# Moving the last pair's gates behind the down products of pair 14, and building the first pair's tokens by a one-hot product

## The chip, the cores and the metric

The kernel runs on one core of a Trainium2 chip. The metric is the device time of one launch in microseconds (us); the median of several runs is used. The core's engines are TensorE (PE; its weight loads are shown as PEld), VectorE (DVE), ScalarE (ACT), GpSimd (POOL) and SyncE (SP), and 16 DMA engines move data between HBM, SBUF and back. Each engine works through its own program in order; a wait on a semaphore holds up all that stands behind it on that engine.

## What is computed

One layer of a hybrid decoder on 320 tokens (256 of a prompt, 64 of eight short samples): a norm, a mixer (convolution group and state-space group), a residual, then a norm and a two-level mixture of experts, a residual and a final norm. The part that this change touches is the mixture of experts. Cut to that, in float32 throughout:

```python
def hier_moe(h, rg_w, rg_b, re_w, re_b, w_gate, w_up, w_down):
    lg = tf @ rg_w + rg_b                                # 4 groups
    grp = argmax(lg); g1 = softmax(lg)[grp]
    le = (tf @ re_w + re_b)[grp]                         # 8 experts of that group
    top_v, top_i = top_k(le, 2); g2 = softmax(top_v)
    eid = grp * 8 + top_i
    combine = sum(one_hot(eid, 32) * (g1 * g2))
    for e in range(32):
        hid = silu(t @ w_gate[e]) * (t @ w_up[e])        # 1024 -> 512
        acc = acc + combine[:, e:e + 1] * (hid @ w_down[e])   # 512 -> 1024
```

## The kernel before

**Tiling.** The tokens are three tiles of 128, 128 and 64 rows (TILES). Experts are worked in 16 pairs (pair i holds experts 2i and 2i + 1). Each expert takes up to 64 of its tokens, so a pair fills 128 rows. For one pair: POOL gathers the normed rows of its 128 slots from HBM (hn_scratch) by an index column; PE transposes them (tokens_T, L1196) into two PSUM banks and DVE multiplies them by the norm's gain into xgt; PE makes the gate and up products of both experts (gate_up, L1213 and L1214, eight k each); ACT takes the silu (L1581), DVE multiplies (L1654); PE transposes the product (hidden_T, L1225), ACT copies it (L1599); PE makes the down products (L1236; the very last expert in halves, L1246), ACT copies their rows into yo (rows_back, L1587); PE adds them to the tokens' places with a one-hot matrix (to_tile, L1261; combine_most has five tiles of six, combine_rest the last).

**Order on PE.** In iteration i stand: gates 2i, combine_most(i - 2), gates 2i + 1, tokens of pair i + 1, combine_rest(i - 2), downs of pair i - 1, hidden_T(i). After the loop come combine 14, then the downs of experts 30 and 31 and the last adds. So the downs of pair 14 stand behind the gates of pair 15.

**Weights.** SP loads 96 blocks of 2 MB (gate, up or down of one expert) in the order of expert_units() into 11 places (e_slot), round and round. Block j may be loaded once block j - 11 is used (gu_done, dn_done). The first eleven lie where the mixer's data lay, so their loads wait for the end of that: block 7 for the out product of the samples (filled, outs), block 8 for the last router logits (lg2), the two halves of block 9 for the normed rows being in HBM (hn_out) and the first gather being issued (gath_begun), block 10 for kept, the last residual rows that PE reads from the same place. Blocks 11 and 12 are loaded in halves, the first halves when half of the first gate product is through (gu_half).

**Choice of experts.** DVE finds the group and the two experts by first_max (maximum, equality times a descending count, maximum, equality). Then "chosen" lets PE count the tokens of each expert (counts, L1157) into the bank "rank". From these DVE makes `first`, a one-hot matrix of tokens against the 128 slots of pair 0, PE multiplies it by the token numbers (L1172), DVE makes an index of it and POOL gathers pair 0. Meanwhile DVE computes the weights and osel, PE the indices of all other pairs (slot_values, L1180), which DVE reads into gpair and others.

**Banks.** MOE_JOBS lists the PSUM jobs of the experts in order; job n lies in bank n mod 3 and waits until job n - 3 has been read.

## Time and profile before

| | before |
|---|---|
| median of 3 runs | 792.37 us (791.98 to 793.82) |
| span of the profiled execution | 789.4 us |
| PE busy | 757.8 us (96%) |
| DVE / ACT / POOL busy | 270.5 / 154.4 / 140.3 us |
| moved by DMA | 249.58 MB, mean 316 GB/s |

The span is the time from the first to the last instruction in the profile of one execution. PE's busy share is that of pipelined matmuls with modelled ends. The clock column ("PEclk") is the clock that was granted to PE, 1.00 for 2.4 GHz and 0.50 for 1.2 GHz. Idle time of an engine is given with what ended it; "issue" stands where the profile shows no releaser.

### The profile page before, as it was taken

The numbers are of one execution on the slowest core, as the hardware profiler recorded it, in microseconds if no ns is written. First come the engines' busy times: TensorE is split into PE (matmuls) and PEld (weight loads), VectorE is DVE, ScalarE is ACT, GpSimd is POOL, SyncE is SP. The second block draws the span as 40 slices with busy tenths as digits, with TensorE's granted clock in tenths as the row PEclk, the third lists the DMA queues.
The fourth block names the chain that finished last, engine by engine and source line by source line (L and its number), as shares of the span: only waits on it lengthen the run. The fifth ranks groups of instructions, "written<-read, shape, count | busy, mean of one in ns | idle before, by whom it ended". The sixth has DMA issues, their size and how long they took to land.

```text
span 789.4 us, 8694 instructions
## 1 busy us (share of the span) xinstructions
PE 757.8 (96%) x3470; PEld 360.5 (46%) x3470; DVE 270.5 (34%) x629; ACT 154.4 (20%) x308; POOL 140.3 (18%) x168
## 2 busy tenths in 40 slices
PE   6999999999999999799999999999999999989896
PEld 4667677767843335434333333333333333333332
DVE  2399499985656423511101101110110011011003
ACT  3211121245712003202011112101111110110122
POOL 2279998612002000100000000000000000000000
PEclk9999999999999999799999999999999999999998
DMA  9990610042659786999999999999999999999982
GB/s 312 304 364 10 230 40 1 9 107 108 188 213 275 252 306 237 368 374 414 429 426 427 425 429 425 425 430 426 427 427 426 425 426 427 427 429 425 429 356 69
DMA packets 51400, 249.58 MB, mean 316 GB/s; under 512 B 6982, under 2 KB 24422, under 8 KB 38671
## 3 DMA queue, kind: packets, MB, share of 16 engines
q1 hardware_dynamic: 45460, 243.40, 77.2%
q10 hardware_dynamic: 3371, 2.81, 1.2%
q0 software_dynamic: 2528, 2.79, 1.1%
q8 instruction: 29, 0.48, 0.2%
q14 instruction: 12, 0.10, 0.0%
HBM read 246.87 MB, written 8.61 MB: 324 GB/s over the span
## 4 chain that ended last, share of the span: by engine, by line
PE 91%; DMA 3%; DVE 2%; SPq 2%; issue 2%; ACT 1%; POOLq 0%; DVEq 0%
PE bank L1213 28%; PE bank L810 18%; PE bank L1236 14%; PE bank L1076 9%; PE bank L1261 9%; DMA xcx<-in_state_conf_conv 2%; PE bank L1196 2%; SPq L491 1%; PE bank L1225 1%; PE bank L1065 1%; PE bank L1034 1%; PE bank L905 1%; PE bank L1214 1%; PE bank L1122 1%; PE bank L1047 0%
## 5 line engine op out<-in xcount | busy, mean ns | idle before, releaser
L810 PE MATMUL bank<-region_a,ring 128*128 128x320 f32 x576 | 157.2, 433 | 1.0 <-DMA ring<-in_w_in 1.0
L1654 DVE TENSOR_TENSOR region_a<-region_a,bank 64x512 f32<-64x512 f32 (+1 forms) x33 | 22.5, 680 | 377.6 <-ACT region_a L1581 377.6
L1214 PE MATMUL bank<-ring,zz 128*64 128x512 f32 x320 | 145.4, 610 | 0.0
L1213 PE MATMUL bank<-ring,zz 128*64 128x512 f32 x288 | 127.3, 595 | 2.7 <-issue 2.7
L810 PEld LDWEIGHTS bank<-region_a,ring 128*128 128x128 f32 x576 | 108.7, 190 | 46.3 <-DVE region_a L1654 1.1
L1655 DVE SCALAR_TENSOR_TENSOR bank<-region_a,par,bank 128x256 f32<-128x256 f32 x232 | 91.2, 479 | 0.0
L763 POOL DMA_INDIRECT region_a<-hn_scratch,region_a x16 | 15.9, 996 | 369.6 <-PE bank L1196 355.8
L1261 PE MATMUL bank<-zz,masks 128*128 128x512 f32 (+1 forms) x192 | 77.2, 603 | 0.7 <-ACT zz L1587 0.7
L1213 PEld LDWEIGHTS bank<-ring,zz 128*64 128x64 f32 x288 | 38.1, 137 | 82.5 <-issue 81.7
L1076 PE MATMUL bank<-ring,x_v_y 128*128 128x512 f32 (+1 forms) x192 | 74.0, 605 | 0.0
L1581 ACT ACTIVATE region_a<-bank 64x512 f32<-64x512 f32 x32 | 18.9, 590 | 271.5 <-PE bank L1214 271.5
L1587 ACT ACTIVATE zz<-bank 64x512 f32<-64x512 f32 x60 | 35.5, 591 | 106.7 <-PE bank L1236 106.3
L1236 PE MATMUL bank<-ring,xcx 128*64 128x512 f32 x240 | 53.8, 596 | 0.0
L1076 PEld LDWEIGHTS bank<-ring,x_v_y 128*128 128x128 f32 (+1 forms) x192 | 26.7, 171 | 43.3 <-issue 43.0
L1261 PEld LDWEIGHTS bank<-zz,masks 128*128 128x128 f32 (+1 forms) x192 | 26.6, 172 | 39.1 <-issue 39.1
L1214 PEld LDWEIGHTS bank<-ring,zz 128*64 128x64 f32 x320 | 43.4, 140 | 0.0
L674 POOL TENSOR_TENSOR x_v_y<-x_v_y 128x512 f32<-128x512 f32 x29 | 36.8, 1270 | 2.3
L1213 PE MATMUL bank<-x_v_y,zz 128*64 128x512 f32 x80 | 35.4, 595 | 0.5 <-issue 0.5
L1236 PEld LDWEIGHTS bank<-ring,xcx 128*64 128x64 f32 x240 | 16.5, 137 | 35.8 <-issue 35.8
L1213 PE MATMUL bank<-xcx,zz 128*64 128x512 f32 x64 | 30.8, 638 | 2.0 <-issue 2.0
L672 POOL TENSOR_TENSOR x_v_y<-region_a,par 128x512 f32<-128x512 f32 x30 | 32.2, 1074 | 2.2
L1214 PE MATMUL bank<-x_v_y,zz 128*64 128x512 f32 x64 | 28.3, 595 | 0.0
(313 smaller groups left out, 770.1 us busy)
## 6 DMA issues: line engine op xcount, KB each, us to landing
ring<-in_expert_w_up SPq DMA_DIRECT2D x20, 2048.0 KB, 24.4
ring<-in_expert_w_gate SPq DMA_DIRECT2D x17, 2048.0 KB, 30.3
ring<-in_expert_w_down SPq DMA_DIRECT2D x16, 2048.0 KB, 34.8
ring<-in_w_in SPq DMA_DIRECT2D x9, 2048.0 KB, 15.7
x_v_y<-in_expert_w_down SPq DMA_DIRECT2D x6, 2048.0 KB, 33.5
x_v_y<-in_expert_w_gate SPq DMA_DIRECT2D x5, 2048.0 KB, 34.6
ring<-in_w_out SPq DMA_DIRECT2D x4, 2048.0 KB, 10.0
xcx<-in_expert_w_gate SPq DMA_DIRECT2D x4, 2048.0 KB, 31.8
```

The costliest lines, as they stand in the source:

```text
L672: link(pool.tensor_tensor(tmp4, u_seq[:, :, :, k:k + TB], w4(par, k, NC), ALU.mult))
L674: return link(pool.tensor_tensor(acc, acc, tmp4, ALU.add))
L810: ins = pe.matmul(pt[0:m, 0:T], w[:, k, :], ht[:, k, :], start=k == 0, stop=k == KD - 1)
L1076: return pe.matmul(dst, mix, w, start=c == 0, stop=c == 2 * NC - 1)
L1213: pe.matmul(to[0:CAP, :], x[:, k, :], wg[:, FE * k:FE * k + FE], **st)
L1214: ins = pe.matmul(to[CAP:P, :], x[:, k, :], wu[:, FE * k:FE * k + FE], **st)
L1236: ins = pe.matmul(to[CAP * q:CAP * q + CAP, :], x[:, k, :], wd[:, D * k + 512 * q:D * k + 512 * q + 512], start=k == 0, stop=k == 3)
L1261: return pe.matmul(dst, rows[:, t0:t0 + n], of[q][0:rows.shape[0], :], start=False, stop=end)
L1581: act.activation(sil[b], job_bank("gate", e)[0:CAP, :], ACT.Silu).then_inc(S("sil"), 1)
L1587: ins = act.activation(yo[own_half[e % 2], 512 * q:512 * q + 512], pt[CAP * q:CAP * q + CAP, :], ACT.Copy)
L1654: tt_ = lambda out, a, b, op: dve.tensor_tensor(out, a, b, op)
L1655: stt = lambda out, a, s_, b, op0, op1: dve.scalar_tensor_tensor(out=out, in0=a, scalar=s_, in1=b, op0=op0, op1=op1)
```

## The change

There are two groups of edits. In the tail, iteration 15 is taken out of PE's loop: after hidden_T(14) come combine 13, the downs of pair 14, combine 14, then the gates of pair 15, hidden_T(15) and the last downs. ACT's order, the order of the weight blocks and the list of bank jobs follow. The four gate and up blocks of pair 15 are loaded in halves, and a gate product waits for the second halves at k = 4 only.

In front, pair 0 is no longer gathered. PE multiplies the normed rows hn (in SBUF) by the one-hot `first`: for each of eight k and three token tiles one product of 128x128. The job "first" goes, and "slots" gets bank 1; all expert jobs lie two banks further. SP loads the second half of block 9 before it waits for lg2, and the first half behind hn_out and xg_T 2. residual(1, [1]) moves ahead of the product. On DVE, three small operations in first_max become two, the subtractions for the two exponentials come after "chosen", osel is made before the weights, and the tokens of pair 0 are scaled before the indices are read. tee and osel move to another place in SBUF.

```diff
@@ expert_units
-        units += [(m, 2 * i + j) for j in range(2) for m in range(2)]
-        if i:
-            units += [(2, 2 * i - 2), (2, 2 * i - 1)]
+        downs = [(2, 2 * i - 2), (2, 2 * i - 1)] if i else []
+        gates = [(m, 2 * i + j) for j in range(2) for m in range(2)]
+        units += downs + gates if i == LAST else gates + downs
@@ SP
-            sp_.wait_ge(filled, J[("lg2",)] + 1)
-            load_expert(n_slot - 3)
...
+            load_half(n_slot - 2, 1, S("tenth_half"))
+            sp_.wait_ge(filled, J[("lg2",)] + 1)
+            load_expert(n_slot - 3)
             sp_.wait_ge(S("hn_out"), 48)
-            load_half(n_slot - 2, 0, S("tenth_half"))
-            sp_.wait_ge(S("gath_begun"), 1)
-            load_half(n_slot - 2, 1, expert_in[n_slot - 2])
+            sp_.wait_ge(S("xg_T"), 2)
+            load_half(n_slot - 2, 0, expert_in[n_slot - 2])
             sp_.wait_ge(S("kept"), 1)
             load_expert(n_slot - 1)
...
+            for e in (NE - 2, NE - 1):
+                pair_of = (E_AT[0, e], E_AT[1, e])
+                for j in pair_of:
+                    place_free(j)
+                    load_half(j, 0, S(f"late_half{e % 2}"))
+                for j in pair_of:
+                    load_half(j, 1, expert_in[j % n_slot])
@@ POOL
-            for i in range(NE // 2):
-                wait(pool, S("xg_T"), 2 * i)
+            for i in range(1, NE // 2):
+                if i > 1:
+                    pool.wait_ge(S("xg_T"), 2 * i)
@@ PE, front
-            pe.wait_ge(S("first"), 1)
-            pt = take(pe, "first")
-            for r in range(3):
-                n = TILES[r][1]
-                ins = pe.matmul(pt[:, 0:1], first[0:n, r, :], tokid[0:n, r:r + 1], start=r == 0, stop=r == 2)
-            ins.then_inc(filled, 1)
             residual(1, [1]).then_inc(S("kept"), 1)
+            pe.wait_ge(S("hn"), 3)
+            pe.wait_ge(S("first"), 1)
+            after_read(pe, "h2", 2, 1)
+            after_read(pe, "lg2")
+            for h in range(2):
+                to = job_bank("tokens", (0, h))
+                for k in range(4):
+                    for r in range(3):
+                        n = TILES[r][1]
+                        ins = pe.matmul(to[:, P * k:P * k + P], hn[0:n, r, 4 * h + k:D:KD], first[0:n, r, :],
+                                        start=r == 0, stop=r == 2)
+                ins.then_inc(S("xg_T"), 1)
@@ PE, tail
+            combine_most(LAST - 2)
+            combine_rest(LAST - 2)
+            expert_down(NE - 4)
+            expert_down(NE - 3)
+            combine_most(LAST - 1)
+            combine_rest(LAST - 1)
+            for e in (NE - 2, NE - 1):
+                pe.wait_ge(S(f"late_half{e % 2}"), 32)
+                gate, up = (e_slot[E_AT[m, e] % n_slot] for m in range(2))
+                to = job_free(pe, "gate", e)
+                pe.wait_ge(S("xgt"), 2 * LAST + 2)
+                gate_up(to, xgt[:, :, own_half[e % 2]], gate, up, late=e).then_inc(S("gu_done"), 1)
+            hidden_T(LAST)
             over = pe.value_load(mcount[0:1, 0:1], min_val=0, max_val=T)
@@ ACT
             for i in range(NE // 2):
+                if i == LAST:
+                    rows_back(2 * i - 2)
+                    rows_back(2 * i - 1)
                 silu(2 * i)
                 silu(2 * i + 1)
-                if i:
+                if 0 < i < LAST:
@@ DVE, first_max
-                for r in range(3):
-                    ins = stt(tmp_[:, r, :], vals[:, r, :], col(mx)[:, r:r + 1], desc, ALU.is_equal, ALU.mult)
-                link(ins)
+                link(tt_(tmp_, vals, wide(mx, w), ALU.is_equal))
+                link(tt_(tmp_, tmp_, bc(desc.unsqueeze(1), [P, 3, w]), ALU.mult))
```

The program order on PE in front, from the counts (s_chosen) to the first gate product. Before:

```order
L1157 MATMUL bank<-region_a,masks 128x96 [waits s_dve_read,s_chosen]
...
L1147 MATMUL bank<-x_v_y,ident 64x512 [waits s_x2]
...
L1172 MATMUL bank<-region_a,zz 128x1 [waits s_dve_read,s_first]
L1172 MATMUL bank<-region_a,zz 128x1 x2
L1147 MATMUL bank<-x_v_y,ident 128x512 [waits s_x2]
L1180 MATMUL bank<-region_a,zz 64x64 [waits s_dve_read,s_osel]
L1180 MATMUL bank<-region_a,zz 64x64 x11
L1196 MATMUL bank<-ident,region_a 128x128 [waits s_gath,s_act_read,s_dve_read]
L1196 MATMUL bank<-ident,region_a 128x128 x7
L1213 MATMUL bank<-xcx,zz 64x512 [waits s_expert_in1,s_xgt,s_expert_in0,s_dve_read]
```

And in the changed kernel (all lines are some 10 to 20 further down):

```order
L1167 MATMUL bank<-region_a,masks 128x96 [waits s_dve_read,s_chosen]
...
L1190 MATMUL bank<-zz,x_v_y 128x128 [waits s_dve_read,s_first,s_hn]
L1190 MATMUL bank<-zz,x_v_y 128x128 x23
L1198 MATMUL bank<-region_a,zz 64x64 [waits s_dve_read,s_osel]
L1198 MATMUL bank<-region_a,zz 64x64 x11
L1233 MATMUL bank<-xcx,zz 64x512 [waits s_expert_in1,s_expert_in0,s_xgt,s_dve_read,s_act_read]
```

The one-column product and the 8 transposes are gone; 24 products of 128x128 stand ahead of the slots product, and both residual products ahead of these.

On SP at the same place, blocks 7 to 10 and the first of block 11. Before:

```order
L503 DMA ring<-in_expert_w_up 128x4096 [waits s_filled]
L503 DMA region_a<-in_expert_w_down 128x4096 [waits s_filled]
L561 DMA x_v_y<-in_expert_w_down 128x2048 [waits s_hn_out]
L561 DMA x_v_y<-in_expert_w_down 128x2048 [waits s_gath_begun]
L503 DMA x_v_y<-in_expert_w_gate 128x4096 [waits s_kept]
L561 DMA xcx<-in_expert_w_up 128x2048 [waits s_gu_half]
```

In the changed kernel:

```order
L506 DMA ring<-in_expert_w_up 128x4096 [waits s_filled]
L562 DMA x_v_y<-in_expert_w_down 128x2048
L506 DMA region_a<-in_expert_w_down 128x4096 [waits s_filled]
L562 DMA x_v_y<-in_expert_w_down 128x2048 [waits s_xg_T,s_hn_out]
L506 DMA x_v_y<-in_expert_w_gate 128x4096 [waits s_kept]
L562 DMA xcx<-in_expert_w_up 128x2048 [waits s_gu_half]
```

One half of block 9 moved ahead of block 8, the other waits for the token product, and block 10 stands behind it.

On PE in the tail, from hidden_T(14) on; L1225 is hidden_T, L1213 a gate product, L1261 a combine, L1236 and L1246 downs. Before:

```order
L1225 MATMUL bank<-ident,region_a 128x128 x3
L1213 MATMUL bank<-xcx,zz 64x512 [waits s_yo,s_xgt,s_expert_in1,s_expert_in0]
...
L1213 MATMUL bank<-ring,zz 64x512 [waits s_yo,s_xgt,s_expert_in3,s_expert_in2]
...
L1236 MATMUL bank<-region_b,xcx 64x512 [waits s_hidt,s_expert_in4]
...
L1236 MATMUL bank<-ring,xcx 64x512 [waits s_hid,s_hidt,s_expert_in5]
...
L1225 MATMUL bank<-ident,region_a 128x128 [waits s_hid]
...
L1261 MATMUL bank<-zz,masks 64x512 [waits s_yo,s_places]
...
L1308 TENSOR_LOAD region_a
...
L1236 MATMUL bank<-ring,xcx 64x512 [waits s_yo,s_hidt,s_expert_in6]
```

In the changed kernel, with L1245 for hidden_T, L1233 for a gate product, L1281 for a combine, L1256 for downs:

```order
L1245 MATMUL bank<-ident,region_a 128x128 x3
L1281 MATMUL bank<-zz,masks 64x512 [waits s_yo,s_places]
...
L1256 MATMUL bank<-xcx 64x512 [waits s_yo,s_hidt,s_expert_in0]
...
L1256 MATMUL bank<-ring,xcx 64x512 [waits s_yo,s_hidt,s_expert_in1]
...
L1281 MATMUL bank<-zz,masks 64x512 [waits s_yo,s_places]
...
L1233 MATMUL bank<-ring,zz 64x512 [waits s_xgt,s_hidt,s_late_half0]
...
L1233 MATMUL bank<-region_b,zz 64x512 [waits s_xgt,s_yo,s_late_half1]
...
L1245 MATMUL bank<-ident,region_a 128x128 [waits s_hid,s_yo]
...
L1336 TENSOR_LOAD region_a
...
L1256 MATMUL bank<-ring,xcx 64x512 [waits s_hid,s_hidt,s_expert_in6]
```

The gates of pair 15 moved behind the downs of pair 14 and combine 14, and nothing but hidden_T and a register load stands between them and the last downs.

## Rows read from the trace of the kernel before

**Rows 1.** The page: DMA busy tenths in 40 slices; the software queue (gathers).

```profile
DMA  9990610042659786999999999999999999999982
...
q0 software_dynamic: 2528, 2.79, 1.1%
```

**Rows 2.** Stretches: us, PE, PEld, DVE, ACT, POOL busy; PEclk, DMA share, GB/s.

```profile
313.00:325.50 12.50, 9.68 (x62) 6.76 (x61) 8.58 (x41) 5.58 (x8) 0.22 (x1) 0.96 0.94 357
...
326.00:328.00 2.00, 1.83 (x2) 0.25 (x2) 1.80 (x9) 0.00 (x0) 0.98 (x1) 0.50 0.83 233
328.00:337.00 9.00, 7.73 (x48) 4.53 (x50) 3.05 (x14) 0.00 (x0) 1.24 (x3) 0.62 1.03 421
337.00:340.50 3.50, 3.50 (x20) 1.29 (x18) 0.00 (x0) 0.00 (x0) 0.00 (x0) 1.00 0.67 186
340.50:360.00 19.50, 18.50 (x91) 7.69 (x88) 3.71 (x6) 2.37 (x4) 0.99 (x1) 1.00 1.01 413
360.00:640.00 280.00, 279.59 (x1235) 100.40 (x1232) 32.32 (x54) 41.99 (x71) 10.82 (x11) 1.00 1.01 426
640.00:762.00 122.00, 114.96 (x490) 41.65 (x488) 11.15 (x19) 16.80 (x29) 2.04 (x3) 0.97 1.01 427
```

**Rows 3.** Timeline: start, us, engine, line; first gate records behind waits.

```profile
648.75 1.00 PE L1213 MATMUL bank<-region_b,zz 128*64 128x512 f32 x1 [1.90 <-issue]
...
708.37 0.61 PE L1213 MATMUL bank<-ring,zz 128*64 128x512 f32 x1 [2.69 <-issue]
...
737.73 1.09 PE L1213 MATMUL bank<-xcx,zz 128*64 128x512 f32 x1 [1.99 <-issue]
```

**Rows 4.** DMA issues at 696.07: the up block of expert 30, us to landing.

```profile
ring<-in_expert_w_up SPq DMA_DIRECT2D x1, 2048.0 KB, 41.6
```

**Rows 5.** Timeline and one line's view: hand-overs and register load in the tail.

```profile
735.11 1.19 ACT L1587 ACTIVATE zz<-bank 64x512 f32<-64x512 f32 x2 [2.24 <-PE bank L1236]
...
757.12 0.59 ACT L1581 ACTIVATE region_a<-bank 64x512 f32<-64x512 f32 x1 [10.07 <-PE bank L1214]
757.74 0.69 DVE L1654 TENSOR_TENSOR region_a<-region_a,bank 64x512 f32<-64x512 f32 x1 [9.90 <-ACT region_a L1581]
...
765.19 1.19 ACT L1587 ACTIVATE zz<-bank 64x512 f32<-64x512 f32 x2 [2.24 <-PE bank L1236]
766.41 0.60 ACT L1599 ACTIVATE xcx<-bank 128x512 f32<-128x512 f32 x1
766.53 4.71 PE L1261 MATMUL bank<-zz,masks 128*64 128x512 f32 x12 [0.70 <-ACT zz L1587]
...
L1308 PEldq TENSOR_LOAD <-region_a x1: 481/481/481, 766.6 to 766.6; - x1
```

**Rows 6.** Timeline in front: choice, counts, residual, SP's loads, first gate.

```profile
318.85 0.50 DVE L1655 SCALAR_TENSOR_TENSOR region_a<-region_a 128x8 f32<-128x8 f32 x3
...
321.00 1.10 DVE L1654 TENSOR_TENSOR region_a<-region_a 128x24 f32<-128x24 f32 x6
...
321.82 1.66 PE L1157 MATMUL bank<-region_a,masks 128*128 128x96 f32 x12 [2.59 <-DVE region_a L1654]
323.41 1.08 PE L1147 MATMUL bank<-x_v_y,ident 64*64 64x512 f32 x4
...
325.21 3.38 SPq L561 DMA_DIRECT2D x_v_y<-in_expert_w_down  x2
...
332.95 1.09 PE L1213 MATMUL bank<-xcx,zz 128*64 128x512 f32 x1
...
337.54 0.33 SPq L561 DMA_DIRECT2D xcx<-in_expert_w_up  x1
```

**Rows 7.** Groups by line and shape, PE, 195 to 240 us: busy us, mean ns.

```profile
L1034 PE MATMUL bank<-ident,ring 128*128 128x128 f32 x64 | 7.6, 275 | 0.8 <-DVE x_v_y L1813 0.8
...
L1013 PE MATMUL bank<-xcx,ring 128*128 128x128 f32 x16 | 1.9, 275 | 0.0
```

**Rows 8.** One stretch, columns as in Rows 2.

```profile
738.00:740.50 2.50, 2.50 (x8) 0.73 (x7) 0.00 (x0) 0.00 (x0) 0.00 (x0) 0.50 1.00 426
```

More of the change, by code:

```diff
@@ L147, in bank_table @@
     fixed = {("yos",): 2, ("mean",): 3, ("h2", 2, 0): 1, ("h2", 2, 1): 2, ("lg2",): 0, ("rank",): 1,
-             ("first",): 0, ("slots",): 2}
+             ("slots",): 1}
     aside = {J[("mean",)]: [("mean",)], J[("h0T", 0, 0)]: [("yos",)], J[("yoT",)]: OUT_JOBS, J[("h2", 0, 0)]: [("lg",)]}
-    for name in (("h2", 2, 0), ("h2", 2, 1), ("lg2",), ("rank",), ("first",), ("slots",)):
+    for name in (("h2", 2, 0), ("h2", 2, 1), ("lg2",), ("rank",), ("slots",)):
         aside[J[name]] = [name]
@@ L188, in moe_jobs @@
     for i in range(NE // 2):
+        jobs += down(i - 1) if i == LAST else []
         jobs += [("gate", 2 * i + j, "hid", 2 * i + j + 1) for j in range(2)]
-        jobs += tokens(i + 1) if i + 1 < NE // 2 else []
-        jobs += down(i - 1) if i else []
+        jobs += tokens(i + 1) if i < LAST else []
+        jobs += down(i - 1) if 0 < i < LAST else []
         jobs += [("hidden", i, "hidt", i + 1)]
@@ L1185, in _ @@
             pe.wait_ge(S("osel"), 1)
-            slot_values(take(pe, "slots")).then_inc(filled, 1)
-            after_read(pe, "first")
+            slot_values(take(pe, "slots"), osel).then_inc(filled, 1)
             pe.wait_ge(free["act"], len([1 for _, who in JOBS if who == "act"]))
@@ L1212, in gate_up @@
                         pe.wait_ge(S("xgt"), 2)
+                    if late is not None and k == 4:
+                        expert_landed(pe, 0, late)
+                        expert_landed(pe, 1, late)
                     pe.matmul(to[0:CAP, :], x[:, k, :], wg[:, FE * k:FE * k + FE], **st)
@@ L1294, in _ @@
                     gate_up(to, xgt[:, :, own_half[e % 2]], gate, up, first=e == 0).then_inc(S("gu_done"), 1)
-                more = i + 1 < NE // 2
-                if more:
-                    pe.wait_ge(S("gath"), 16 * (i + 2))
-                    for h in range(2):
-                        tokens_T(i + 1, h)
+                pe.wait_ge(S("gath"), 16 * (i + 1))
+                for h in range(2):
+                    tokens_T(i + 1, h)
                 if i >= 2:
@@ L1967, in _, with tokens @@
             link(tt_(col(M_W2), col(M_W1), col(M_E), ALU.mult))
[L1968 to L1979 removed]
+            tt_(val[:, :, :, 1, :], ee, bc(cols[:, M_W1:M_W2 + 1, :].unsqueeze(3), [P, 2, 3, NE]), ALU.mult)\
+                .then_inc(S("osel"), 1)
+            def tokens(i, h):
+                dve.wait_ge(S("xg_T"), 2 * i + h + 1)
+                src = job_bank("tokens", (i, h))
+                tt_(xgt[:, 4 * h:4 * h + 4, :], src[:, :].rearrange("p (k s) -> p k s", k=4),
+                    bc(lnffn[:, 4 * h:4 * h + 4].unsqueeze(2), [P, 4, P]), ALU.mult).then_inc(S("xgt"), 1)
+            for h in range(2):
+                tokens(0, h)
             link(dve.tensor_reduce(cols[:, M_T, 0:1], cnt, AX.X, ALU.max))
@@ L2017, in tokens_more @@
                            bc(lnffn[:, :].unsqueeze(2), [P, KD, CAP]), ALU.mult)
-            for h in range(2):
-                tokens(0, h)
             def places(b, tok, w):
```

76 lines of the change are left out of this document (31 added, 45 removed).

## The prediction

> **What bounds the kernel now.** I read the slices of the page first. From the 18th slice on the DMA engines stand at 9 of 10 and never leave it until the last weights are in [rows 1]. The table of stretches gives the rate: 426 and 427 GB/s from 360 to 762 us [rows 2]. One pair of experts needs six weight blocks of 2.10 MB, 12.6 MB, so 29.5 us. TensorE (PE) is busy nearly all the time too, so the second question is which of the two waits. Until 640 us it is not PE: 279.59 of 280 us busy [rows 2]. Behind that its idle times come before the first gate product of a pair, 1.90 us at 648.75, 2.69 at 708.37 and 1.99 at 737.73, with "issue" as releaser, which is how a wait for a landed weight block looks here [rows 3]. The starts at 708.37 and 737.73 lie 29.36 us apart, the time of one pair on the DMA engines. So from 646 us on the weight stream sets the pace, and whatever delays the stream in the first 340 us delays 708.37 by as much, since there is no gap in it afterwards to make it up. After 737.73 nothing waits for a weight again, and PE's own work and its hand-overs with ACT and DVE set the end. Check of the reading: the up block of expert 30 is issued at 696.07 and lands 41.6 us later, at 737.7 [rows 4].
>
> Two places therefore count: how early the stream is without holes (312 to 340 us), and PE's chain from 735.7 us on. The edits are costed as what they do to these two.
>
> **Front: the choice.** Each of the three first_max calls swaps three small operations in one group (0.50 us) for two that wait for each other, about 0.18 + 0.04 us each [rows 6]: 0.44 instead of 0.53 with its gap, 0.27 us over three. Two subtractions of 3 or 12 columns leave the path to "chosen", about 0.1 us each, as they ran back to back with their neighbours. For the six in a row at 321.00 that is 1.10/6 = 0.18 as an upper bound [rows 6]. PE's counts, at 321.82 before [rows 6], start near 321.35.
>
> **Front: the tokens of pair 0.** The gather, 3.8 us from issue, the 8 transposes and the one-column product go. In their place stand 24 products of 128x128 in float32, three token tiles for each of eight k. Nearest row: L1013, non-transposed float32 128x128, two records to a matmul, 16 records in 1.9 us, so 0.119 a record [rows 7]. 48 records are 5.7 us at full clock. Ahead of them PE does the counts (1.6 us from 321.82 to 323.41 [rows 6]), residual(2) (1.08 with its tail, about 1.0 to the next [rows 6]) and now also residual(1, [1]), which is two more steps of 512 columns like those two, 0.9 us. The one-hot is two DVE operations behind the counts, under 1 us by the gap from 323.41 to PE's next work before, so DVE is ready before PE is. Product: from 321.35 + 1.6 + 1.0 + 0.9 = 324.8 to 330.5. Slots product (24 records, 1.0 to 1.7 us), which the gates wait for, then about 1.3 us of DVE reads: gates start near 333.0, as before (332.95 [rows 6]), but without the half clock that before had from 325.5 on [rows 2]. PE has 1.9 us of slack at 648.75 anyway, so this start is covered, and pays only from 2 us of delay on.
>
> A page of the Trainium skill has a rule against this trade. TensorE: Matmul & The Clock Gate, Terms, says that transpose mode makes float32 four times as fast as a matmul. The transposes L1034 take 0.119 us each and the matmuls L1013 0.238 [rows 7], a factor of two here, so the trace does not bear the rule out.
>
> **Front: the stream.** This is the term that matters. SP now issues the second half of block 9 right behind block 7 (312.2), no longer behind hn_out and the gather's start. But the first half now waits for xg_T 2, the end of the product, because it lands on the normed rows that the product reads. Block 10 stands behind it in SP's queue though its own condition is met earlier. Their issue was at 325.21 and right after 328.1; it becomes 330.6 for both. Bytes moved by 340.5 us, before: 12.5 us x 357 + 2 x 233 + 9 x 421 + 3.5 x 186 GB/s = 4.46 + 0.47 + 3.79 + 0.65 = 9.37 MB [rows 2], less one gather of 2.79/16 = 0.17 MB [rows 1], 9.2 MB. After: blocks 7, 8, half of 9 and the last hn rows, 5.5 MB, done near 327; then nothing until the restart. What a restart costs I take from 325.21: no packet before 326.0, then 233 GB/s for 2 us, a lag of 0.8 + 0.9 = 1.7 us. So as if at full rate from 332.3; (340.5 - 332.3) x 0.427 = 3.5 MB, sum 9.0 MB. The second restart of before (337.54 [rows 6], 186 GB/s) is gone: half a block and block 10 last until 339.8, and the next halves, bound to half of the first gate product, are issued near 336.6. The lack of 0.2 to 0.3 MB at 427 GB/s is **+0.6 us**. Bounds: a ramp half as long, DVE a little faster and a gather hidden give -0.4; a chain later by 0.5 us and restarts as before give +1.5.
>
> **Tail: what goes.** Order before from 735.74: wait 1.99 for the blocks of expert 30, gates 30 (low clock at first), combine 13 and gates 31, downs 28 and 29, hand-over 0.70, combine 14 and downs 30 and 31. The same products stand in the new order, so they cancel. Removed: the wait 1.99 [rows 3]; the low clock, 737.7 to 741.0 at 0.50 [rows 8], where 3.3 us give 1.65 us of work, so 1.65; the wait 0.70 before combine 14 with 0.07 beside it [rows 5]. Sum 4.4 us.
>
> **Tail: what comes.** (a) combine 13 now follows the downs 26 and 27 at once and needs their rows, which ACT copies from 735.11 to 736.30 [rows 5]; PE starts 0.15 later, as at 766.53. Wait 0.7. (b) combine 14 stands directly behind downs 28 and 29: 765.19 to 766.53 plus 0.02 [rows 5], 1.36, with no hidden transposes in it to cover a part. (c) hidden_T(15) directly behind gates 31: silu 0.59 from 757.12, DVE 0.69 to 758.43 [rows 5], 1.45 us that the downs used to cover. (d) ACT's copy of the hidden rows, 0.60 [rows 5], before down 30: 0.75, formerly under combine 14. Beside it stands PE's register load, 0.48 us and two short steps [rows 5], about 0.85 from its start before; it overlaps (d) and adds 0 to 0.2. Sum 4.3 us. The weights: downs 28 and 29 take the queue places of gate and up 30, whose second block landed at 737.7 [rows 4]; the gates take the next, up to 747.5 for 30 and 757.3 for 31, at 4.9 us a block, and are needed near 754 and 761. So the loading in halves buys nothing here and costs nothing; SP is far ahead (landing takes over 40 us). **Tail: -0.1, call it 0.** Bounds: -1.5 if (a) costs nothing and (b) only the 0.70 of before [rows 5], +0.5 if the register load shows.
>
> **Sum.** 789.4 + 0.6 + 0 = 790.0 us of span. The median of the runs, 792.37, is 3.0 us above the profiled span, so **793.0 us**. A change within 0.2%, 1.6 us, can't be told from none here.
>
> **Rivals.** (1) The clock falls where it matters; this ends slower. Before, it was at half from 325.5 us [rows 2], behind 2.59 us of idle [rows 6] and small products, and the gates found it so. Should it fall in the new product for a stretch like that at 737.7, 3.3 us, only 1.65 us of work is done in it, and the stream restarts 1.7 us later: 794.7. The same price stands in the tail: (c) and (d) leave PE with only four transposes in 2.9 us, right before the downs 30 and 31, and 1.99 us of idle was enough at 737.73, whose first record took 1.09 us, while 2.69 us at 708.37 was not, 0.61 [rows 3]. [...] The low stretch in before's tail is one of these throws as well; a median run may not have it. For either of the two 0.33 (794.7), for both 0.07 (796.4). The Trainium skill, TensorE: Matmul & The Clock Gate, The HAM clock gate, has the throttled state as the default that activity must release; the low rows behind idle agree.
>
> (2) The product is dearer than L1013, since its rows are read at a stride of 8. If it took 0.48 us a matmul, 24 take 11.4 us, the stream comes 5.7 us later and the gates too: 798.7. Chance 0.05; the strided transposes of before give no sign of it. The skill's factor of four (same page, Terms) would give just this.
>
> (3) Faster. The holes in the stream shrink more than I count and the hand-overs overlap: -0.4 and -1.5 in place of +0.6 and 0, so 792.37 - 1.9 = 790.5. It decides if the product ends before 329 us. Chance 0.17. (4) The forecast, 792.2 to 793.9: 0.38.
>
> **Numbers.** Faster by over 0.2% (below 790.8): most of (3), 0.13. Within: the forecast, the rest of (3), some of (1) that falls on a lucky side, 0.47. Slower (above 794.0): 0.40, from (1) and (2). Range: 790.4 to 796.2; below it lies less than half of (3), about 0.07, above it both falls of the clock and (2), about 0.12.
>
> **What would show it.** Right: token product near 324.8 to 330.5 with 48 records; SP's halves and block 10 together at 330.6; DMA silent 327 to 331.4, then no second hole; the first gate of pair 14 at about 709.0; PE waits of about 0.7, 1.4, 1.5 and 0.8 us in the tail and none for weights. Wrong: a product of over 7 us, weight waits behind 737, or a start of pair 14 before 708.

## The result, and the profile after

The changed kernel took **806.99 us** (median of 4 runs, 805.31 to 807.34), the kernel before 793.1 us beside it: a ratio of 1.0164 with a 95% interval of 1.0137 to 1.0191. It is 13 to 14 us slower, outside the range of the prediction. The profiled execution has a span of 805.2 us against 789.4, so 15.8 us are to be found. That is 2 us more than the medians differ by: the changed kernel's profiled execution took 807.0 us, 1.8 more than its span, so by estimate the profiled execution of before took 791.2, under its median.

In the page's 40 slices the DMA engines now drop to 3 of 10 in the 17th slice, where they stood at 9 [rows 1]; the clock is down there too, and again near the end:

```profile
PEclk9999999999999999789999999999999999989999
DMA  9990610044477886399999999999999999999971
```

The stretches of [rows 2] in the kernel after, with the same columns:

```profile
326.00:328.00 2.00, 2.00 (x9) 1.76 (x8) 1.58 (x8) 0.00 (x0) 0.00 (x0) 1.00 0.91 389
328.00:337.00 9.00, 9.00 (x30) 7.40 (x29) 0.69 (x1) 0.00 (x0) 0.00 (x0) 0.68 0.01 4
337.00:340.50 3.50, 3.50 (x12) 2.61 (x11) 0.00 (x0) 0.00 (x0) 0.00 (x0) 0.50 0.00 0
340.50:360.00 19.50, 18.14 (x91) 7.39 (x90) 2.78 (x13) 0.59 (x1) 1.09 (x1) 0.80 0.88 348
...
640.00:762.00 122.00, 114.12 (x480) 41.59 (x482) 11.88 (x20) 17.15 (x29) 2.96 (x3) 0.97 1.01 426
```

Between 328 and 340.5 us nothing to speak of is loaded and PE is busy without a gap. With what, its timeline says (start, us, line; a row joins records that follow each other); it answers to [rows 6]:

```profile
322.36 1.66 PE L1167 MATMUL bank<-region_a,masks 128*128 128x96 f32 x12 [0.43 <-DVE region_a L1685]
323.95 2.13 PE L1157 MATMUL bank<-x_v_y,ident 64*64 64x512 f32 x6
325.92 15.43 PE L1190 MATMUL bank<-zz,x_v_y 128*128 128x128 f32 x48
341.28 1.74 PE L1198 MATMUL bank<-region_a,zz 128*64 128x64 f32 x24
344.38 1.08 PE L1233 MATMUL bank<-xcx,zz 128*64 128x512 f32 x1 [1.36 <-issue]
```

The token product, 48 records, takes 15.43 us where 5.7 were counted, and the gates start at 344.38 instead of 332.95. SP's rows show its loads behind it: both held ones at once when the product ends, the next halves at 350.02 (before: 337.54 [rows 6]):

```profile
341.42 0.33 SPq L562 DMA_DIRECT2D x_v_y<-in_expert_w_down  x1
341.79 0.43 SPq L506 DMA_DIRECT2D x_v_y<-in_expert_w_gate  x1
350.02 0.33 SPq L562 DMA_DIRECT2D xcx<-in_expert_w_up  x1
```

Three hundred microseconds on, the first gate records behind waits, which answer to [rows 3], and then the hand-overs of the new tail, which answer to [rows 5]:

```profile
660.80 0.61 PE L1233 MATMUL bank<-region_b,zz 128*64 128x512 f32 x1 [1.47 <-issue]
...
721.25 1.08 PE L1233 MATMUL bank<-ring,zz 128*64 128x512 f32 x1 [2.66 <-issue]
...
752.30 4.71 PE L1281 MATMUL bank<-zz,masks 128*64 128x512 f32 x12 [0.70 <-ACT zz L1615]
...
765.41 4.71 PE L1281 MATMUL bank<-zz,masks 128*64 128x512 f32 x12 [1.38 <-ACT zz L1615]
...
785.51 0.72 PE L1245 MATMUL bank<-ident,region_a 128*128 128x128 f32 x4 [1.50 <-DVE region_a L1685]
786.97 3.65 PE L1256 MATMUL bank<-ring,xcx 128*64 128x512 f32 x16 [0.73 <-ACT xcx L1630]
```

The whole difference stands in two places. The first gate of pair 14 starts at 721.25 instead of 708.37: **12.9 us**, all of it handed on from the front. From there to the end it is 83.95 us instead of 81.03: **2.9 us**. The sum is 15.8. The weights' rate (426 GB/s) is what it was; the delay arises in the front, and the rows of the end only show it. Four waits in the tail come out as counted (0.70, 1.38, 1.50, 0.73; counted 0.7, 1.36, 1.45, 0.75). New is that pair 14's first record takes 1.08 us instead of 0.61: the clock is at half there, 0.50 from 721 to 727 in

```profile
721.00:727.00 6.00, 5.75 (x14) 1.92 (x16) 0.00 (x0) 0.00 (x0) 0.00 (x0) 0.50 1.01 429
```

### The profile page after: what moved, and what is told of

Same layout as the page of the kernel before. It is cut to its first block, busy times and chain, and to the rows that moved or that the text cites. A ratio compares the mean times of both kernels' runs of the same rounds, so it can differ in the third digit from the quotient of the medians.

```text
span 805.2 us, 8758 instructions
## 1 busy us (share of the span) xinstructions
PE 772.9 (96%) x3504; PEld 372.1 (46%) x3504; DVE 272.1 (34%) x625; ACT 154.5 (19%) x308; POOL 139.1 (17%) x166
## 4 chain that ended last, share of the span: by engine, by line
PE 74%; DVE 4%; issue 2%; ACT 1%; DVEq 0%
PE bank L1233 28%; PE bank L1256 14%; PE bank L1086 9%; PE bank L1281 9%; PE bank L1190 2%; PE bank L1213 2%; PE bank L1245 1%; DVE bank L1686 1%; PE bank L820 1%; PE bank L1075 1%; PE bank L1044 1%; PE bank L915 1%; DVE x_v_y L1686 1%; PE bank L1234 1%; DVE bank L1724 1%
## 5 line engine op out<-in xcount | busy, mean ns | idle before, releaser
L820 PE MATMUL bank<-region_a,ring 128*128 128x320 f32 x576 | 158.9, 437 | 1.2 <-DMA ring<-in_w_in 1.2
L1685 DVE TENSOR_TENSOR region_a<-region_a,bank 64x512 f32<-64x512 f32 x32 | 22.1, 691 | 393.9 <-ACT region_a L1609 393.9
L1234 PE MATMUL bank<-ring,zz 128*64 128x512 f32 x320 | 145.9, 611 | 0.0
L1233 PE MATMUL bank<-ring,zz 128*64 128x512 f32 x288 | 130.3, 606 | 2.7 <-issue 2.7
L1281 PE MATMUL bank<-zz,masks 128*128 128x512 f32 (+1 forms) x192 | 76.9, 602 | 2.1 <-ACT zz L1615 2.1
L1233 PEld LDWEIGHTS bank<-ring,zz 128*64 128x64 f32 x288 | 38.8, 139 | 84.9 <-issue 84.1
L1256 PE MATMUL bank<-ring,xcx 128*64 128x512 f32 x240 | 53.8, 595 | 0.7 <-ACT xcx L1630 0.7
L1281 PEld LDWEIGHTS bank<-zz,masks 128*128 128x128 f32 (+1 forms) x192 | 26.5, 172 | 40.4 <-issue 40.4
L1233 PE MATMUL bank<-x_v_y,zz 128*64 128x512 f32 x80 | 35.4, 595 | 3.0 <-issue 3.0
L1256 PEld LDWEIGHTS bank<-ring,xcx 128*64 128x64 f32 x240 | 16.7, 137 | 35.7 <-issue 35.7
L1233 PE MATMUL bank<-region_b,zz 128*64 128x512 f32 x64 | 28.2, 594 | 2.1 <-issue 1.5
```

The costliest lines, as they stand in the source:

```text
L820: ins = pe.matmul(pt[0:m, 0:T], w[:, k, :], ht[:, k, :], start=k == 0, stop=k == KD - 1)
L1233: pe.matmul(to[0:CAP, :], x[:, k, :], wg[:, FE * k:FE * k + FE], **st)
L1234: ins = pe.matmul(to[CAP:P, :], x[:, k, :], wu[:, FE * k:FE * k + FE], **st)
L1256: ins = pe.matmul(to[CAP * q:CAP * q + CAP, :], x[:, k, :], wd[:, D * k + 512 * q:D * k + 512 * q + 512], start=k == 0, stop=k == 3)
L1281: return pe.matmul(dst, rows[:, t0:t0 + n], of[q][0:rows.shape[0], :], start=False, stop=end)
L1685: tt_ = lambda out, a, b, op: dve.tensor_tensor(out, a, b, op)
```

## Which half of the change costs the time

Two runs undo one part each. The first keeps the front of before and takes the tail of the change; its diff is the tail part of the diff shown ahead. The second is the reverse.

> The kernel before with only the tail part of the change (downs 28 and 29 and combine 14 ahead of gates 30 and 31, those blocks loaded in halves, a hidden_T of its own at the end); choice, token gather and front as before. My theory (all of the loss is in the front, the tail is worth 0): first gate of pair 14 at about 708.4 on the scale of the profile of before, waits in the tail of about 0.7, 1.4, 1.5 and 0.7 us, time within 1.5 us of before (791.5 to 794.5). Rival (the tail edit itself costs, for example by a low clock that it brings): 795 or more, with the waits or a low stretch of 6 us behind pair 14's first gates to be seen.

> The changed kernel with the tail part undone (gates of pair 15 where they were, whole blocks); the front is that of the change. My theory: product of 48 records in about 15.4 us, blocks 9a and 10 issued near 341.5, weight waits of the last pairs 12.9 us later than before; time 792.4 + 12.9 = 805.3, with the low clock of 6.6 us at pair 14's gates perhaps another 1.5: 805 to 807. Rival (the tail carries part of the loss): 803 or less.

Measured: the tail alone 795.8 us, ratio to before 1.0034 (1.0012 to 1.0056); the front alone 806.7 us, 1.0153 (1.0118 to 1.0188). The front carries the bulk, as my theory had it. The tail isn't worth 0, though: e1 lies above the range I gave for it and meets its rival (795 or more). Behind the slow front the tail's part can't be told from none: 1.0164 for the whole change against 1.0153 for the front alone. The first gate of pair 14 and the last hand-over of e1, with the downs of expert 30 behind it:

```profile
709.45 1.09 PE L1227 MATMUL bank<-ring,zz 128*64 128x512 f32 x1 [2.54 <-issue]
...
773.66 5.35 PE L1250 MATMUL bank<-ring,xcx 128*64 128x512 f32 x16 [0.73 <-ACT xcx L1627]
```

The clock is at half at both places: the 16 records at 773.66 take 5.35 us, where the changed kernel took 3.65. More on this below.

## What makes the product slow

The product takes normed rows as its stationary operand in steps of 8 elements. The next runs store them in another order, so that each 128 columns lie side by side, and change nothing else in the product; gathered rows are read that way too.

```
-                act.activation(hn[0:n, r, :], xt[0:n, r, :], ACT.Copy, scale=rst[...])
+                act.activation(hn[0:n, r, :].rearrange("p (k j) -> p k j", k=KD),
+                               xt[0:n, r, :].rearrange("p (j k) -> p k j", k=KD), ACT.Copy, scale=rst[...])
...
-    ins = pe.matmul(to[...], hn[0:n, r, 4 * h + k:D:KD], first[0:n, r, :], ...)
+    ins = pe.matmul(to[...], hn[0:n, r, P * (4 * h + k):P * (4 * h + k) + P], first[0:n, r, :], ...)
```

> The changed kernel, but ACT writes the normed rows with the columns in order of k (8 groups of 128), so that each 128 columns that the product takes as its stationary operand are contiguous, as are those of the gathered rows' transposes. My theory (the stride of 8 in the stationary operand sets the product's pace): 48 records at 0.12 us, 5.7 us at full clock and up to 7 with a low clock in it, SP released at 331.5 to 333 instead of 341.4, stream 9 to 10 us earlier, time 796 to 798. Rival (non-transposed float32 products of this shape or the falling clock make it slow, not the stride): still over 11 us for the product and 803 or more. Second rival (ACT's strided write becomes dear): the hn event comes later than 325 us.

> As the run before with the normed rows in order of k, and with the tail part of the change undone. My theory: as the run before, 795 to 798, the tail worth under 1.5 us either way. It is also the candidate for beating both: if the holes in the weight stream shrink as forecast it ends near 793; rival: at the time of the kernel before minus 2.

Measured: 797.21 us, 1.0044 (1.0019 to 1.0069), and with the tail of before 796.89 us, 1.0024 (0.9998 to 1.005). About 10 us come back by the order of the columns alone. The second rival (the write becomes dear) did not decide: ACT's three writes took 2.15 to 2.25 us each in place of 1.15, but the last ended at 320.7 us and the product began at 328.2. The rows of PE's weight loads explain the gain. First the changed kernel, then e3 (line, engine, operation, count: min/median/max in ns):

```profile
L1190 PEld LDWEIGHTS bank<-zz,x_v_y x48: 308/335/340, 325.5 to 340.7; 128*128 128x128 f32 x32, 64*128 64x128 f32 x16
```

```profile
L1190 PEld LDWEIGHTS bank<-zz,x_v_y x47: 183/189/192, 328.2 to 336.2; 128*128 128x128 f32 x31, 64*128 64x128 f32 x16
```

335 ns against 189. The starts tell more than the durations, since a load overlaps the next one: where the rows' number stays the same, loads follow each other 0.11 us apart in e3 and 0.24 in the changed kernel. The clock doesn't make that difference. It was at full until past 331 us and at half behind it; two stretches of records, one at each level (13 records are 12 steps, 19 are 18):

```profile
L1190 PE MATMUL bank<-zz,x_v_y x13: 400/403/606, 327.5 to 331.1; 128*128 128x128 f32 x9, 64*128 64x128 f32 x4
```

```profile
L1190 PE MATMUL bank<-zz,x_v_y x19: 442/449/607, 333.2 to 339.2; 128*128 128x128 f32 x13, 64*128 64x128 f32 x6
```

That is 0.30 us a record at full clock and 0.34 at half. So the rival of the falling clock is out as the main cause; over the 30 records from 331.1 us on it made about 1.0 us. But e3's product still took 8.42 us and not 5.7:

```profile
328.20 8.42 PE L1190 MATMUL bank<-zz,x_v_y 128*128 128x128 f32 x48
```

Its clock was at full all through, and its loads were as long as those of L1013 (192 ns). What is left is that every third step has 64 rows instead of 128: the third token tile. In the code's order PE changes between the two 16 times.

```
             for h in range(2):
                 to = job_bank("tokens", (0, h))
-                for k in range(4):
-                    for r in range(3):
-                        n = TILES[r][1]
+                for r in range(3):
+                    n = TILES[r][1]
+                    for k in range(4):
...
-                                        start=r == 0, stop=r == 2)
+                                        start=r + k == 0, stop=r == 2 and k == 3)
```

> The changed kernel with one thing altered: inside a bank the loop over the three token tiles stands outside and that over the four k inside, so PE changes between records of 128 rows and of 64 rows 4 times in the product instead of 16. The run before (contiguous) showed 48 records in 8.42 us and not 5.4 to 5.7, although its weight loads took as long as those of L1013. Theory: a change of the rows' number costs about 0.1 us on each of the two records behind it; then this product, still at the stride of 8, takes about 2.4 us less: 12.5 to 13.2 us instead of 15.4, time 804 to 805. Rival (the stride alone, and what is above 0.112 a record in the contiguous run comes from start and stop or from two records of one accumulation): still 15.4 us and 807.

Measured: 804.31 us, 1.0131 (1.0094 to 1.0167). Its product, still at the stride of 8:

```profile
329.02 12.22 PE L1190 MATMUL bank<-zz,x_v_y 128*128 128x128 f32 x48
```

15.43 became 12.22 us for 12 changes fewer, 0.27 us a change; in the contiguous form (e9, below) 8.42 became 6.10, 0.19 a change. The difference of the two prices is the clock, not the stride. e5's loads between changes step by 0.24 us at half clock too (15 of them, 14 steps, in 3.4 us, at 0.50):

```profile
L1190 PEld LDWEIGHTS bank<-zz,x_v_y x15: 337/338/338, 329.0 to 332.4; 128*128 128x128 f32 x15
```

Six records of the changed kernel hold two changes and took 1.82 us at full clock and 2.03 at half; less six steps of 0.24, a change cost 0.19 us at full and 0.29 at half. The sum then closes on the 15.4 us: 5.4 for 48 contiguous records at 0.112, 6.1 for the stride (e9's 6.10 against e5's 12.22), 2.9 for 15 changes at 0.19, 1.0 for the low clock. From which stride it is dear, the next run asks:

> The changed kernel, but the product's stationary operand is read at a stride of 1, 1, 2, 2, 4, 4, 8 and 8 elements for its eight k, so the tokens of pair 0 are other values than they should be; the number and shape of the records is the same. Theory (the stride sets the load): a weight load of 0.19 us at stride 1 and 0.31 to 0.34 at stride 8, with the middle steps telling from which stride it is dear; the product takes 9 to 13 us. Rival (any stride but 1 costs the same): 12 of 48 loads at 0.19, the other 36 at 0.31 to 0.34, about 13.5 us.

The product took 12.11 us, the kernel 804.75 us in its one run. Loads of the eight k in order, two at a stride of 1, two at 2, two at 4, two at 8:

```profile
L1191 PEld LDWEIGHTS bank<-zz,x_v_y x12: 183/190/192, 328.4 to 330.5; 128*128 128x128 f32 x8, 64*128 64x128 f32 x4
...
L1191 PEld LDWEIGHTS bank<-zz,x_v_y x11: 189/196/197, 330.8 to 332.6; 128*128 128x128 f32 x8, 64*128 64x128 f32 x3
...
L1191 PEld LDWEIGHTS bank<-zz,x_v_y x10: 304/329/332, 333.2 to 336.1; 128*128 128x128 f32 x7, 64*128 64x128 f32 x3
...
L1191 PEld LDWEIGHTS bank<-zz,x_v_y x10: 309/338/340, 337.0 to 340.1; 128*128 128x128 f32 x7, 64*128 64x128 f32 x3
```

190, 196, 329, 338 ns: a step between 2 and 4 elements of float32. The rival (any stride but 1) is refuted. The Trainium skill, SBUF — State Buffer, Door 1, says that SBUF is read in lines of 16 bytes and that two hits to a line are needed for the full rate; two float32 to a line are a stride of 2, one is a stride of 4, and that is where the step lies. The same passage puts the stride that is still free at 4 float32; e6 has 329 ns there, so this figure doesn't hold here. The Trainium skill, TensorEngine Tiling (Array Packing), Key Properties, has a change of tiling mode drain the engine. Whether a step from 128 to 64 rows is such a change it doesn't say; the price of one would fit. Neither rule was weighed ahead of the run, and that they are the reason for the two prices is not shown.

## Who hands the delay on

The prediction saw two ways out of the product: SP's held loads, and the gates. This run takes SP's wait away by having the product read something else.

```
             sp_.wait_ge(S("hn_out"), 48)
-            sp_.wait_ge(S("xg_T"), 2)
             load_half(n_slot - 2, 0, expert_in[n_slot - 2])
...
-            pe.wait_ge(S("hn"), 3)
+            pe.wait_ge(expert_in[0], 16)
...
-    ins = pe.matmul(to[...], hn[0:n, r, 4 * h + k:D:KD], first[0:n, r, :], ...)
+    ins = pe.matmul(to[...], e_slot[0][0:n, 4 * h + k + D * r:D * r + D:KD], first[0:n, r, :], ...)
```

> The changed kernel, but the product reads the loaded weights of expert block 0 at a stride of 8 in place of the normed rows, and SP no longer waits for the end of the product; the tokens of pair 0 are therefore wrong. The slow product itself (about 15.4 us) stays and the gates start as late as in the changed kernel. Theory (the loss is that of the weight stream, held by SP's wait): blocks 9a and 10 issued near 326, weight waits of the last pairs near those of before, so at most 3 us later; but PE starts the gates 11.4 us later and has only 1.9 us of slack at 648.75, of which 4.6 in all until pair 14, so PE's own chain becomes the bound: 799 to 802. Rival (the wait of SP is harmless, the late gates alone set the loss): 806 to 807, with the gates never waiting for weights.

Measured: 807.57 us, 1.0165 (1.0125 to 1.0206), as slow as the changed kernel. My theory fell, the rival that I had put beside it stands, but for one point: PE does wait for weights. Its loads and a stretch behind them:

```profile
324.92 0.33 SPq L562 DMA_DIRECT2D x_v_y<-in_expert_w_down  x1
326.80 0.33 SPq L506 DMA_DIRECT2D x_v_y<-in_expert_w_gate  x1
350.79 0.33 SPq L562 DMA_DIRECT2D xcx<-in_expert_w_up  x1
```

```profile
340.50:350.50 10.00, 8.64 (x46) 4.44 (x47) 2.09 (x12) 0.00 (x0) 1.09 (x1) 0.57 0.04 9
...
661.63 0.61 PE L1232 MATMUL bank<-region_b,zz 128*64 128x512 f32 x1 [1.52 <-issue]
```

Block 9a was issued 16.5 us and block 10 15.0 us earlier than in the changed kernel. Then all slots were full, and the DMA engines stood still until the first half of the first gate product released one, at 350.79. The hole only moved. The release of slots ties the stream to the start of the gates, whatever was loaded before it. The kernels with one release of first halves all fit this. From the release of the first half (gu_half) to the first gate record of the last pairs that had to wait for weights (648.75 in the kernel before) it is 310.3 to 311.7 us in each of them:

| kernel | SP's release | first weight wait ends | difference |
|---|---|---|---|
| before | 337.54 | 648.75 | 311.21 |
| e1 tail only | 338.91 | 650.09 | 311.18 |
| e9 contiguous, rows outside | 339.63 | 650.77 | 311.14 |
| e8 the same with a part of block 10 early | 340.05 | 651.39 | 311.34 |
| e12 tail, whole blocks | 342.99 | 653.96 | 310.97 |
| e4 contiguous, old tail | 343.70 | 654.02 | 310.32 |
| e3 contiguous | 344.35 | 655.54 | 311.19 |
| changed | 350.02 | 660.80 | 310.78 |
| e6 strides | 350.12 | 661.86 | 311.74 |
| e5 rows outside | 350.25 | 660.99 | 310.74 |
| e7 unheld | 350.79 | 661.63 | 310.84 |
| e2 front only | 353.42 | 664.29 | 310.87 |

Two kernels with both cures test the same thing from the other side. Both have contiguous rows, token tiles outside and the tail of before; e8 also loads what of block 10 doesn't lie on the normed rows as soon as the residuals are done.

```
             sp_.wait_ge(S("hn_out"), 48)
+            sp_.wait_ge(S("kept"), 1)
+            load_part(n_slot - 1, 0, 3 * D, S("eleventh_part"))
             sp_.wait_ge(S("xg_T"), 2)
             load_half(n_slot - 2, 0, expert_in[n_slot - 2])
-            sp_.wait_ge(S("kept"), 1)
-            load_expert(n_slot - 1)
+            load_part(n_slot - 1, 3 * D, UNIT, expert_in[n_slot - 1])
```

> The front of the changed kernel with three alterations, its tail part undone: normed rows contiguous in k; the token tiles outside in the product; and of block 10 the first 3072 columns, which do not lie on the normed rows, loaded as soon as the residuals are done, the rest and block 9a behind the product. My theory: product of 5.4 us plus four changes of shape, 6 us; blocks 9a and the rest of 10 issued about 332; hardly a hole in the weight stream between 328 and 333; about 4 us of stream gained on the contiguous run, so 792 to 793, between 3 us faster and equal to before. Rival (what is left of the loss in the contiguous runs lies elsewhere, before the product): 796 or more.

> The run e8_contig_rows_part without its early piece of block 10: front of the change, normed rows contiguous, token tiles outside, old tail; SP again waits for the end of the product before block 10. New theory, formed on e7_unheld: SP's issue of blocks 9a and 10 sets nothing, since all slots are full soon after and SP then waits for the first half of the first gate product (gu_half); the loss is handed on by the gates' start alone. So the time is that of e8_contig_rows_part, 793 to 794.5, and the first weight wait of the last pairs ends 311 us behind SP's issue of the next halves. Rival (the empty DMA engines from 328 to 332 cost what they lack): 4.5 us less product, yet 3 us more than e8: 796 to 797.

Measured: e8 793.67 us, 1.0012 (0.9993 to 1.0032); e9 793.02 us, 0.9995 (0.9975 to 1.0014). Both are 13 to 14 us faster than the changed kernel and can't be told from the kernel before. The rival to e9 (the empty DMA engines cost what they lack, 796 to 797) is refuted. In e9:

```profile
327.49 6.10 PE L1180 MATMUL bank<-zz,x_v_y 128*128 128x128 f32 x48
...
335.94 0.61 PE L1220 MATMUL bank<-xcx,zz 128*64 128x512 f32 x1 [1.36 <-issue]
```

```profile
328.00:337.00 9.00, 7.64 (x75) 6.47 (x76) 3.97 (x19) 0.00 (x0) 1.08 (x1) 1.00 0.33 110
337.00:340.50 3.50, 3.50 (x19) 1.38 (x16) 0.00 (x0) 0.00 (x0) 0.02 (x1) 1.00 1.04 439
```

110 GB/s in a stretch where the kernel before moved 421 [rows 2], nine microseconds long, and it costs nothing that the times can tell: the empty DMA engines that I had costed in the prediction are not on the path. The gates of e9 start 3.0 us later than before but at full clock, so the release comes only 2.1 us later.

From this I expected that an earlier release would gain time, and asked for it in two kernels: the first halves in two quarters, the first as soon as two of eight k are done.

```
-            sp_.wait_ge(S("gu_half"), 1)
-            for j in (n_slot, n_slot + 1):
-                load_half(j, 0, S("first_halves"))
+            for q in range(2):
+                sp_.wait_ge(S("gu_half"), q + 1)
+                for j in (n_slot, n_slot + 1):
+                    (quarter q of block j, to S("first_halves"))
...
-                    if first and k == 3:
+                    if first and k in (1, 3):
                         ins.then_inc(S("gu_half"), 1)
```

> The kernel before with one thing altered: the first halves of the two blocks behind the first eleven are loaded in two quarters each, the first as soon as two of the eight k of the first gate product are done instead of four. New theory (that release sets the whole weight stream behind it): the quarter is issued about 1.7 to 2.5 us earlier, the hole from 337 to 340.5 closes, first weight wait of the last pairs ends about 1.7 to 2 us earlier than 648.75 on the scale of the profile of before, time 790.5 to 791.5. Rival (the release sets nothing, other things do): as before.

> The run e8_contig_rows_part with the same quarters. New theory: release 1.8 us earlier, time 1.5 to 2 less than e8, near 792; it has no low clock in the first gates, which the kernel before has, but starts them 3.4 us later, so it doesn't beat e10. Rival: as e8, 793.7.

Measured: e10 792.45 us, 0.9994 (0.9973 to 1.0015); e11 794.06 us, 1.0011 (0.9989 to 1.0032). No gain can be told in either. The times alone don't exclude the 2 us that I expected, the traces say more. The first wait of the last pairs ends 310.1 us behind the second release in e10, 1 us less than in the kernel before, and 311.7 us in e11. The hole comes back one release later. In e10, from 350 on, before gu_done of the second expert has taken effect:

```profile
340.50:350.00 9.50, 9.50 (x47) 3.23 (x42) 0.69 (x1) 0.59 (x1) 0.00 (x0) 1.00 1.01 395
350.00:355.00 5.00, 3.99 (x24) 2.39 (x26) 2.33 (x4) 1.19 (x2) 0.99 (x1) 1.00 0.90 318
```

The kernel before had 413 GB/s from 350 to 355. e11 is the cleaner test, since its product ends when that of e8 does (334.11 and 334.01): its first quarters are issued at 338.43, 1.6 us ahead of e8's halves, yet the first weight wait ends at 651.82 against e8's 651.39, and from 355 to 360 it moved 382 GB/s where e8 moved 424. So it looks as if not the one release sets the stream but the row of them, which all hang on the gates; no run moved the later releases alone. In e10 the gates also started late, at 335.10, so its first quarters left at 337.98, no earlier than the halves of before (337.54). The gathered rows landed later than in the profile shown ahead:

```profile
333.13 1.94 PE L1198 MATMUL bank<-ident,region_a 128*128 128x128 f32 x8 [3.98 <-DMA region_a<-hn_scratch,region_a]
```

This wait was 0.93 us in the kernel before, 0.73 in e1, 3.98 here and 6.62 in e12. The gather that the change removes has a price that varies from run to run; how much of the spread of the kernel before (790.15 to 797.13 us beside these runs) is due to it was not tested.

## The tail

The last run takes the halves out of the tail.

```
-            for e in (NE - 2, NE - 1):
-                pair_of = (E_AT[0, e], E_AT[1, e])
-                for j in pair_of:
-                    place_free(j)
-                    load_half(j, 0, S(f"late_half{e % 2}"))
-                for j in pair_of:
-                    load_half(j, 1, expert_in[j % n_slot])
+            for j in range(E_AT[0, NE - 2], E_AT[2, NE - 2]):
+                place_free(j)
+                load_expert(j)
...
```

> As e1_tail_only, but the gate and up blocks of pair 15 are loaded whole. Theory (PE waits for no weight in the tail, the loading in halves buys nothing): as e1, 794.5 to 797, no weight wait behind pair 14's first gates. Rival (the halves bring something): 1 us or more slower than e1, with a weight wait before gates 30. What costs the 2.6 us in e1 is by my reading the low clock at pair 14's first gates and behind the hand-overs at the end, which the order brings and which stands or falls from run to run; a mean of 5 rounds shows it again.

Measured: 797.57 us, 1.0048 (1.0028 to 1.0068), beside 1.0034 (1.0012 to 1.0056) of e1. The halves bring nothing that can be measured: the intervals would hide 1 us, but in neither profile does PE wait at the gates of pair 15, whole blocks or halves. The order is what costs. From pair 14's first gate record to the end of the span:

| tail | clock at half (0.50) | us |
|---|---|---|
| old: e10, e11 | at pair 14's gates | 79.4, 79.9 |
| old: before, e2, e4, e9 | at pair 15's gates | 81.0, 81.3, 81.2, 81.1 |
| old: e8 | nowhere | 79.2 |
| new: e5, e6 | nowhere | 80.9, 80.9 |
| new: e3, e12 | at the last downs | 82.5, 82.6 |
| new: changed, e7 | at pair 14's gates | 83.95, 83.7 |
| new: e1 | at both | 84.15 |

In the old order a low clock at pair 14's gates costs next to nothing (79.4 against 79.2), because PE waits for weights once more at pair 15's. In e10:

```profile
709.69 1.09 PE L1215 MATMUL bank<-ring,zz 128*64 128x512 f32 x1 [2.68 <-issue]
...
739.04 0.61 PE L1215 MATMUL bank<-xcx,zz 128*64 128x512 f32 x1 [0.63 <-issue]
```

The wait shrank to 0.63 us and took the loss in; the starts still lie 29.35 us apart. In the new order no weight wait follows, and all of it reaches the end: 3 us in the changed kernel. Without any low clock it is 80.9 against 79.2: the four hand-overs (4.3 us) against 0.7 and a weight wait of about 2.

## Why the prediction was wrong

**Views and bound: right.** The stream sets the pace from 646 us on, and what delays it in the front arrives at 708.37 in full. 12.9 us did.

**The choice: right.** From SP's issue of block 7 (312.24 before, 313.24 after) to the counts it is 9.12 us instead of 9.58; 0.47 were expected. The two residuals took 1.97 us, expected 1.9.

**The tokens of pair 0: the step that failed.** The term was mis-sized by the row it was taken from. "Nearest row: L1013 ... so 0.119 a record" gave 5.7 us; it was 0.32 a record, 15.4 us. L1013 is alike in type, shape and count of records, but its operand lies side by side and all its records have 128 rows. Both differences were in the code and each has its price: 6.1 us for the stride, 2.9 for the changes; the low clock in the product made the last 1.0. Rival (2) had the stride as a mechanism, with a chance of 0.05 and 11.4 us, on the ground that "the strided transposes of before give no sign of it". They did, in the row of the loads, which the prediction doesn't use; it goes by the matmul rows, whose times are alike. Contiguous (L1034) and at a stride of 8 (L1196), both in the kernel before:

```profile
L1034 PEld LDWEIGHTS bank<-ident,ring x64: 138/141/143, 212.2 to 221.3; 128*128 128x128 f32 x64
```

```profile
L1196 PEld LDWEIGHTS bank<-ident,region_a x128: 186/190/226, 331.0 to 726.8; 128*128 128x128 f32 x128
```

With contiguous rows the latter's loads are 137/140/145 ns in e9. A transpose hides 190 ns, so the sign was in the loads alone.

**The stream: wrong in its cause.** This is the second step that failed. I costed the hole from 328 us on by its missing bytes, and called the gates' start covered for the 1.9 us of slack at 648.75. That slack is itself made by the stream, and the stream is tied to the gates: it moves with them. e7 shows SP's wait to be worth nothing, e9 an empty stretch to be worth nothing. By the table of releases the product's excess of 9.7 us, a start 1.1 later than counted (1.0 of it stands already at block 7's issue, ahead of all that the change moves), 0.5 more of hand-over and the low clock in the first half product (5.64 us instead of 4.59) are the 12.5 us of the release, with 0.4 of scatter behind it.

**The clock: rival (1) partly right.** It fell in the product and in the tail. In the product it came not behind idle time, as rival (1) has it, but past 331 us, with PE busy without a gap since 323. In all five kernels whose product reads at strides of up to 8 (changed, e2, e5, e6, e7) it fell to 0.50 in the course of the product, in none of the five with contiguous rows (e3, e4, e8, e9, e11) did it; why isn't shown. It cost little there, about 1.0 us, since the load sets the pace. In the tail it cost 3.0 us (83.95 against 80.9 in e5 and e6) and not 1.65, and it matters in the new order more than in the old, which the prediction had not seen.

**The tail: its four waits right, its sum by luck of one profile.** It was called 0 by counting the low clock of that profile (1.65 us) as removed, and against it the new order without a low clock does come out so (80.9 and 81.0). But that low clock was a throw, as the prediction itself says in rival (1); without it the tail is +1.5, with one of its own it is more, and e1 has +2.7 us (0.34%).

## What to carry to other kernels

Before costing a product by a row of the same shape, compare what the shape doesn't say: the stride of the stationary operand and whether the number of rows changes from record to record; read the weight loads' rows (PEld) beside the matmuls'. Where slots are released by the work that the stream feeds, empty DMA engines are not the loss: follow the chain from the first release. In this kernel a wait further down absorbed a low clock ahead of it; an order that removes the wait removes this cover too.

## What the runs showed of the hardware

A float32 load of 128 columns in a plain product took 190 ns at a stride of 1, 196 at 2, 329 at 4 and 338 at 8 (e6), and at these strides loads of equal rows followed each other 0.11, 0.12, 0.24 and 0.24 us apart. At a stride of 8 that was 0.24 at full clock and at half (e5); contiguous it was 0.11 at full and 0.21 at half (e8). In transposes a load took 140 at 1 and 190 at 8 (e9, before). A change between records of 128 and of 64 rows cost 0.19 us at full clock, with contiguous loads (e3 against e9) and at a stride of 8 (changed kernel), and 0.29 to 0.30 at half clock (changed kernel; e4, contiguous). ACT's write of the normed rows in another order took 2.15 to 2.25 us in place of 1.15 (e3, e9), off the path here. The indirect gather's landing kept PE waiting between 0.73 and 6.62 us in four executions of the same front.
